# First norm's modulation in four quarters, rows of x reloaded earlier, sums on four column groups

## The reference, cut to what matters

```python
def modulate(h, shift, scale):
    return h * (1 + scale) + shift
def adaln(cond, w, b):                       # w_ada: 1024 x 6144, six pieces of 1024 columns
    return jnp.split(jax.nn.silu(cond) @ w + b, 6, axis=-1)

sh1, sc1, g1, sh2, sc2, g2 = adaln(c, w_ada, b_ada)
csh1, csc1, *_ = adaln(c_ctx, w_ada, b_ada)
hc = modulate(rms_norm(ctx, norm_mix), csh1, csc1)        # 256 tokens of context
s_f, s_b = hgrn2_context_states(*split(hc @ w_in[:, 512:2048]), lb_f, lb_b)
hx = modulate(rms_norm(x, norm_mix), sh1, sc1)            # 512 tokens
mx = token_mix(hx, w_in, w_out, ..., s_f, s_b)            # two gated scans and a convolution
x = x + g1 * mx
hx2 = modulate(rms_norm(x, norm_ffn), sh2, sc2)
x = x + g2 * expert_choice_ffn(hx2, w_router, w_gate, w_up, w_down)   # 16 experts
x = rms_norm(x, norm_final)
# second block: u = rmsnorm(x, g_mix); z = u @ w_in_2, of which 24 columns are the gates of the
# attention branches (sigmoid(zg)); then attention, convolution, FFN, a last gate, a last norm
```

## Time and profile before

| | us |
|---|---|
| median of 3 runs (lowest to highest) | 2087.41 (2086.91 to 2089.4) |
| the profiled execution | 2087.24 |
| its span in the trace | 2085.2 |
| PE busy | 1998.8 (96%) |
| DVE busy / ACT busy / POOL busy | 899.3 / 577.0 / 58.2 |
| DMA | 529.58 MB, mean 254 GB/s |

### The profile page before, as it was taken

One profiled execution on the slowest core, in us unless ns is written; L12 is line 12 of the kernel. 1 busy time (PEld: TensorE's weight loads), 2 busy tenths in 40 slices (PEclk: granted clock), 3 DMA queues, 4 the chain that ended last, 5 costly groups with the idle time before them and its releaser, 6 DMA issues.

```text
span 2085.2 us, 23804 instructions
## 1 busy us (share of the span) xinstructions
PE 1998.8 (96%) x9896; PEld 1247.4 (60%) x9896; DVE 899.3 (43%) x1478; ACT 577.0 (28%) x901; POOL 58.2 (3%) x107
## 2 busy tenths in 40 slices
PE   7999999999999899999999888999999999999998
PEld 5888777543533334242423323776688888888886
DVE  4666683320111111111101101877897656767555
ACT  5434322100100000000000001437725343334445
POOL 1000010000000000000000000005300000000000
PEclk9999999999999999999999999999999999999999
DMA  9462127899999999999999999142132232232322
GB/s 353 162 232 91 41 72 292 362 404 406 428 430 430 430 431 413 429 431 430 431 431 430 431 431 419 56 136 41 41 117 86 81 121 81 91 112 81 111 78 84
DMA packets 111099, 529.58 MB, mean 254 GB/s; under 512 B 15397, under 2 KB 44177, under 8 KB 83345
## 3 DMA queue, kind: packets, MB, share of 16 engines
q1 hardware_dynamic: 110993, 528.07, 62.7%
HBM read 525.95 MB, written 2.10 MB: 253 GB/s over the span
## 4 chain that ended last, share of the span: by engine, by line
PE 91%; DMA 4%; DVE 2%; issue 2%; ACT 0%; SPq 0%; POOL 0%; ACTq 0%; DVEq 0%
PE bank L1099 22%; PE bank L646 12%; PE bank L647 12%; PE bank L648 12%; PE bank L1183 9%; PE bank L1056 3%; PE bank L1073 3%; PE bank L653 3%; PE bank L655 3%; PE bank L657 3%; DMA f<-in_w_gate_dram 3%; PE bank L667 2%; PE bank L1288 1%; PE bank L1397 1%; DMA f<-in_w_in_dram 1%
## 5 line engine op out<-in xcount | busy, mean ns | idle before, releaser
L1099 PE MATMUL bank<-f,high 128*64 128x512 f32 x2048 | 463.5, 600 | 31.4 <-issue 15.3
L646 PE MATMUL bank<-r 128*128 128x512 f32 x920 | 363.4, 395 | 3.4 <-DVE r L2114 2.7
L647 PE MATMUL bank<-r 128*128 128x512 f32 x920 | 359.2, 390 | 0.0
L648 PE MATMUL bank<-r 128*128 128x512 f32 x920 | 358.9, 390 | 0.0
L1099 PEld LDWEIGHTS bank<-f,high 128*64 128x64 f32 x2048 | 147.6, 137 | 317.1 <-issue 299.8
L1183 PE MATMUL bank<-f,high 128*64 128x512 f32 x1024 | 227.5, 600 | 8.3 <-issue 8.3
L2454 DVE SCALAR_TENSOR_TENSOR f<-bank,low,f 128x512 f32<-128x512 f32 x64 | 48.0, 750 | 401.6 <-PE bank L1073 401.2
L1529 ACT ACTIVATE high<-bank 128x512 f32<-128x512 f32 (+3 forms) x95 | 52.1, 579 | 564.0 <-PE bank L667 269.8
L408 DVE TENSOR_TENSOR r<-f,r 128x1024 fp32r<-128x1024 f32 (+2 forms) x167 | 190.9, 1196 | 32.2 <-ACT r L402 32.1
L646 PEld LDWEIGHTS bank<-r 128*128 128x128 f32 x920 | 172.3, 187 | 45.8 <-issue 5.5
L648 PEld LDWEIGHTS bank<-r 128*128 128x128 f32 x920 | 172.4, 187 | 37.6
(11 more groups left out here) (397 smaller groups left out, 2059.5 us busy)
## 6 DMA issues: line engine op xcount, KB each, us to landing
f<-in_w_up_dram SPq DMA_DIRECT2D x58, 2048.0 KB, 20.6
f<-in_w_down_dram SPq DMA_DIRECT2D x56, 2048.0 KB, 20.2
f<-in_w_gate_dram SPq DMA_DIRECT2D x55, 2048.0 KB, 19.1
f<-in_w_up_dram SPq DMA_DIRECT2D x34, 1024.0 KB, 7.2
f<-in_w_in_dram SPq DMA_DIRECT2D x13, 2048.0 KB, 7.8
f<-in_w_down_dram SPq DMA_DIRECT2D x22, 1024.0 KB, 10.7
high<-in_w_ada_dram SPq DMA_DIRECT2D x32, 512.0 KB, 5.4
f<-in_w_gate_dram SPq DMA_DIRECT2D x16, 1024.0 KB, 10.0
```

The costliest lines, as they stand in the source:

```text
L646: pe.matmul(o, wh, xh, start=first, stop=False)
L647: pe.matmul(o, wl, xh, start=False, stop=False)
L648: return pe.matmul(o, wh, xl, start=False, stop=last)
L1099: ins = pe.matmul(o[64 * e:64 * e + 64, :], xsT[p % 2][:, 2 * k + r, 64 * e:64 * e + 64], ws[e](2048 * r + 512 * fc), start=k == 0 and r = ...
```

## The change

Five edits, in program order.

1. The modulation's blocks are cut in four quarters q of 256 features: `early[q]` holds scale and shift of the quarter (rows of 1 KB). SP issues for each q a quarter of ZF, scale q, shift q. `ada_columns(q, a)` multiplies 256 columns, `ada_turned(q)` and `modulation(q)` follow. Quarter 0 comes ahead of the loop over k, quarters 1 to 3 in the middle of k = 0, 2 and 4, turned at k = 1, 3 and 5. Three matmuls on ones (256 columns) stand ahead of the loop. ACT and DVE split ZF's first quarter ahead of the copies of x. Chunk VI waits for quarter 2.
2. ACT's context root stands between tiles 5 and the copy of quarter 3; `pt2` moves behind the first token tile by VI; `ctx_state` is cut in `ctx_turned` and `ctx_state`, with a projection between.
3. The rows of x are reloaded in two halves, after DVE's second `gates` and after the second scan's last products, ahead of the last output weights.
4. `route_sums` takes two d at a time, on four column groups; the two halves are added by a matmul with `fold2` in place of the transpose.
5. The 24 gate columns are one plain float32 product on four column groups (`gate_columns`, weights times gain in `WG`), added by a matmul with `fold4`.

```diff
-            load_ada(2)
-            load_ada(0)
-            load_chunk(0)
-            load_ada(3)
-            load_ada(1)
+            for q in range(4):
+                load_chunk(ZF, [q])
+                sp.dma_start(early[q][:, SCALE], ada_part(SCALE, q)).then_inc(s[f"scale{q}"], 16)
+                sp.dma_start(early[q][:, SHIFT], ada_part(SHIFT, q)).then_inc(s[f"shift{q}"], 16)
...
-            sp.wait_ge(s["pe_ada"], val("pe_ada", 3))
-            sp.wait_ge(s["pe_ada"], val("pe_ada", 1))
+            sp.wait_ge(s["pe_ada"], val("pe_ada", 2))
             load_chunk(1)
...
+            sp.wait_ge(s["v_gla"], val("v_gla", "gates", 1))
+            sp.dma_start(xres[:, 0:2, :], x_v[:, 0:2, :]).then_inc(s["x0"], 16)
+            sp.wait_ge(s["pe_scan"], val("pe_scan", 1, 14))
+            sp.dma_start(xres[:, 2:4, :], x_v[:, 2:4, :]).then_inc(s["x1"], 16)
             sp.wait_ge(s[freed(N1 - 3)[0]], val(*freed(N1 - 3)))
             load_chunk(N1 - 1)
...
-            tokens_turned(0)
-            tokens_turned(1)
-            ada_columns(ada_order[0])
-            tokens_turned(2)
-            ada_turned(ada_order[0])
-            ada_columns(ada_order[1])
+            for t in range(3):
+                tokens_turned(t)
+            ada_columns(0, SCALE)
             tokens_turned(3)
-            ada_turned(ada_order[1])
+            ada_columns(0, SHIFT)
+            ada_turned(0)
+            pe.wait_ge(s["consts"], val("consts", "ones256"))
+            after(3)
+            for _ in range(3):
+                pe.matmul(banks[3][:, 0:256], ident, ones256, start=True, stop=True)
...
             for k in range(8):
-                if k == 2:
-                    ada_columns(3, 0)
-                    ada_columns(1, 1)
-                if k == 3:
-                    ada_turned(3, 2)
-                    ada_turned(1, 3)
+                q, odd = k // 2 + 1, k % 2
+                if odd and q < 4:
+                    ada_turned(q, 2)
...
                 for j in range(4):
+                    if j == 2 and not odd and q < 4:
+                        ada_columns(q, SCALE, q % 2)
+                        ada_columns(q, SHIFT)
...
-            for t in range(2):
-                o = take(("vctx", t), "a_proj", "vctx", t)
-                up(project_tokens(o, VI, t, HCH, HCL), "pe_proj", "vctx", t)
+            o = take(("vctx", 0), "a_proj", "vctx", 0)
+            up(project_tokens(o, VI, 0, HCH, HCL), "pe_proj", "vctx", 0)
+            ctx_turned(0)
+            o = take(("vctx", 1), "a_proj", "vctx", 1)
+            up(project_tokens(o, VI, 1, HCH, HCL), "pe_proj", "vctx", 1)
+            ctx_gate(ZB, 1)
             ctx_state(0)
-            ctx_gate(ZB, 1)
...
-            ctx_state(1)
+            ctx_turned(1)
             for h in range(4):
                 o = take(("q", h), "a_proj", "q", h)
                 up(project(o[:, :], QC, h, UH, UL), "pe_proj", "q", h)
+                if h == 0:
+                    ctx_state(1)
...
+            def route_sums(d0):
+
                 pe.wait_ge(s["v_route"], val("v_route", "wrm"))
-                pe.matmul(st1[0:32, :], WRm[:, d, :], XT[:, d, :], start=d == 0, stop=d == 7)
-                up(pe.matmul(st1[32:64, :], onesD[:, 0:32], sq1[d % 2], start=d == 0, stop=d == 7), "pe_sq", 1, d, 0)
+                for d in (d0, d0 + 1):
+                    g = 64 * (d % 2)
+                    pe.wait_ge(s["sq"], val("sq", 1, d, 0))
+                    pe.matmul(st1[g:g + 32, :], WRm[:, d, :], XT[:, d, :], start=d < 2, stop=d > 5)
+                    up(pe.matmul(st1[g + 32:g + 64, :], onesD[:, 0:32], sq1[d % 2], start=d < 2, stop=d > 5), "pe_sq", 1, d, 0)
...
-                for d in ((0, 1), (2, 3), (4,), (5,))[j]:
-                    route_sums(d)
+                if j < 3:
+                    route_sums(2 * j)
             route_sums(6)
-            route_sums(7)
...
-                ins = pe.transpose(o[:, 64 * t:64 * t + 64], sums[:, 128 * t:128 * t + 128], ident[0:64, 0:64])
+                ins = pe.matmul(o[:, 64 * t:64 * t + 64], sums[:, 128 * t:128 * t + 128], fold2, start=True, stop=True)
...
+            def gate_columns():
+
+                o = take(("ct", 2), "a_z", "ct", 2)
+                pe.wait_ge(s["v_z"], val("v_z", "wg"))
+                for r in range(2):
+                    for g in range(4):
+                        ins = pe.matmul(o[32 * g:32 * g + 32, :], WG[:, 2 * g + r, :], XT[:, 2 * g + r, :],
+                                        start=r == 0, stop=r == 1)
+                up(ins, "pe_z", "ct", 2)
...
-            columns(KVG, 256, 24, 2)
+            gate_columns()
...
+            for q in range(4):
+                ada_tmp(q)
+                if q == 0:
+                    a_divide(a, ZF, [1])
+                rounded_tokens((2 * q, 2 * q + 1))
+                if q < 2:
+                    a_divide(a, ZF, [q + 2])
+                if q == 1:
+                    a.wait_ge(s["v_pre"], val("v_pre", "lbd"))
+                    a.activation(lb0, lb0, ACT.Exp)
+                    up(a.activation(lb1, lb1, ACT.Exp), "a_pre", "lbe")
+                if q == 2:
+                    context_root()
             a_divide(a, VI)
...
+            v.wait_ge(s["hi"], val("hi", KVG, 3))
+            up(v.tensor_tensor(WG[:, :, 0:24], v3(whole(KVG)[:, 0:2240], 8)[:, :, 256:280],
+                               gain12.unsqueeze(2).to_broadcast([P, 8, 24]), ALU.mult), "v_z", "wg")
+            own_wait("v_z")
             v_divide(v, KVG)
...
+            ctx_turned(0)
             v_divide(v, ZB)
+            ada_sums(12, 18)
             ctx_state(0)
-            ada_sums(12, 22)
+            ada_sums(18, 22)
```

More of the change, by code:

```diff
@@ L18 @@
 NEG = -1e30
-DMA_SEMS = (*(f"g{i}" for i in range(6)), *(f"cg{i}" for i in range(4)), *(f"zf{i}" for i in range(4)), "x0", "x1", "rows0", "rows", "small", "ctx", "wple", "ada0", "ada1", "ada2", "ada3", "w0", "w1", "ptok", "gf", "out",
+DMA_SEMS = (*(f"g{i}" for i in range(6)), *(f"cg{i}" for i in range(4)), *(f"zf{i}" for i in range(4)), "x0", "x1", "rows0", "rows", "small", "ctx", "wple", *(f"scale{i}" for i in range(4)), *(f"shift{i}" for i in range(4)), "w0", "w1", "ptok", "gf", "out",
             *(f"m{i}" for i in range(9)), "mx", "my", "mg0", "mg1", "mh0", "mh1", "mq0", "mq1")
@@ L121, in build_program @@
         CP = v3(mem(8 * 32), 8)
-        cursor[0] += 96
+        fold2, fold4 = mem(64), mem(24)
+        cursor[0] += 8
         XT_AT = cursor[0]
@@ L411, in build_program @@
         x_v = I["x"][0].rearrange("(t p) d -> p t d", p=P)
[L412 to L414 removed]
+        early = [own(4096, a_).rearrange("p (a k n) -> p a k n", a=2, k=8)
+                 for a_ in (M + 14336, M + 18432, slot_at[2], slot_at[3])]
+        SHIFT, SCALE = range(2)
         def ada_slot(n):
@@ L436, in sync, with load_chunk @@
         def sync(sp):
-            def load_chunk(c):
+            def load_chunk(c, pieces=None):
                 for i, (dst, src) in enumerate(chunks[c][0](whole(c))):
+                    if pieces and i not in pieces:
+                        continue
                     sp.dma_start(dst, src).then_inc(s[{ZF: f"zf{i}", CG: f"cg{i}"}.get(c, f"w{pair[c]}")], 16)
@@ L782, in tensor @@
                        "pe_proj", "cf", t, half)
-            pe.wait_ge(s["rows"], 16 * len(rows1))
-            o = take(("pt2",), "v_pre", "pt2")
-            up(turn_blocks(o, [stage[:, i, :] for i in range(1, 5)]), "pe_pre", "pt2")
             turn["order"], turn["i"] = [4, 5, 6, 7], 0
@@ L789, in tensor @@
                 up(project_tokens(o, VI, t, UH, UL), "pe_proj", "vtok", t)
+                if t == 0:
+                    pe.wait_ge(s["rows"], 16 * len(rows1))
+                    o = claim(0, ("pt2",), "v_pre", "pt2")
+                    up(turn_blocks(o, [stage[:, i, :] for i in range(1, 5)]), "pe_pre", "pt2")
                 if t == 1:
                     ctx_gate(ZF, 0)
-            for t in range(2):
-                o = take(("vctx", t), "a_proj", "vctx", t)
-                up(project_tokens(o, VI, t, HCH, HCL), "pe_proj", "vctx", t)
+            o = take(("vctx", 0), "a_proj", "vctx", 0)
[4 more added lines that the diff above has]
+            ctx_gate(ZB, 1)
             ctx_state(0)
-            ctx_gate(ZB, 1)
             for h in range(4):
@@ L1275, in to_tokens @@
                 for t in range(4):
-                    ins = pe.transpose(o[:, m * t:m * t + m], ct[i][0:m, 128 * t:128 * t + 128], ident[0:m, 0:m])
+                    z = slice(128 * t, 128 * t + 128)
+                    if i < 2:
+                        ins = pe.transpose(o[:, m * t:m * t + m], ct[i][0:m, z], ident[0:m, 0:m])
+                    else:
+                        ins = pe.matmul(o[:, m * t:m * t + m], ct[i][:, z], fold4, start=True, stop=True)
                 up(ins, "pe_z", "tk", i)
@@ L2217, in vector @@
             v_divide(v, VI)
-            v.wait_ge(s["pe_pre"], val("pe_pre", "pt2"))
```

(4 more changed lines are left out.)

204 lines of the change are left out of this document (95 added, 109 removed).

## The result

The changed kernel takes 2076.54 us in the median of four runs (2075.66 to 2076.88), beside 2087.74 for the kernel before in the same session (2086.91 to 2089.4): a ratio of 0.9944, 95% interval 0.9932 to 0.9956, or 11.2 us less. The profiled execution took 2076.56 us, 10.7 less than that of before, and its span is 10.4 shorter.

A forecast was written before the change was run, and what follows sets the result against it. PE was taken as the bound, with 91% of the chain, and DMA near the expert stage's end. Terms -1.0 + 0.5 - 3.0 - 1.8 - 1.2 - 3.1 = -9.6 from 2087.24 (median 2087.41) gave 2077.7; 8-in-10 range 2074.5 to 2082.5.

The forecast's parts named there:

- VI: First norm: chunk VI issued up to 5 us later behind the quarters' rows; value +0.5, bounds 0 and +2.7.
- The step on the clock: First norm: with ones, PE idles 1.3 us; since 1.83 us of idle kept the clock at 1.00, it stays high.
- The price of that fall: First norm: at the low clock, 1.2 GHz, the first eight products cost 1.6 us more.
- The margin at quarter 3: First norm: ACT's copy of quarter 3, behind the context's root, done at 45; PE wants it at 45.8.
- The rival that rested on it, the first rival: First norm gives nothing: root or VI too late, clock falls, +2.5 + 1.5 instead of -0.5; 2082.2, chance 0.16.
- the quarters double the number of rows in the queue: SP's queue at the first norm: more rows, so VI issued up to 5 us later, landing at 46.5 to 52.
- The folds' estimate of 0.93: Router sums and gates: four float32 products of two instructions replace transposes of 0.43, taking 0.93; +0.5 in each part.
- 2.2 us for eight matmuls at that share: Parts 4 and 5: at overlap share 0.79, eight matmuls take 2.2 instead of 1.92; both parts bring 0.5 less.
- The conclusion (it passes shifts on): Expert stage: whatever PE gains before about 470 us moves the transfer stream and its end by as much.
- From there on the stream runs without a gap: Expert stage: after the empty DMA queues at 470 us, the weight stream has no further gap.
- the last rival: More: clock stays high, quarter 0 starts at 23, all waits go in full; 2074, chance 0.06.

The follow-up runs named there:

- nine traces: One trace each of nine profiled kernels sharing the changed kernel's start; first product between 23.66 and 25.14 us, mean 24.53; the loop behind it takes 31.00 to 31.07.
- all but its start: Kernel before with the change's x reload, sums and gate columns, but the old first norm and old context order: 2080.5 us, ratio 0.9967 to the kernel before.
- the early products: Changed kernel with 30 products of the identity with itself ahead of the first parameter rows and 4 behind them: 2074.76 us, ratio 0.9938 to the kernel before.
- the delay ahead of it: Changed kernel with 16 more products on ones (7.2 us) ahead of the second block of output products, at about 345 us: 2083.53 us, ratio 0.9982.
- the delay in pair 3: Changed kernel with the same 7.2 us of extra products on ones put in expert pair 3: 2083.36 us, ratio 0.9976 to the kernel before.

## Why the prediction was right

I forecast 2077.7 in a range of 2074.5 to 2082.5; 2076.54 was measured. Term by term, in us:

| part | forecast | before against after | undone by itself, in the trace |
|---|---|---|---|
| 1, first norm, with VI | -0.5 | -0.3 | not tried alone |
| 2, context | -3.0 | -3.55 | -3.0, without `pt2` |
| 3, rows of x | -1.8 | -1.9 | -3.6 |
| 4, sums | -1.2 | -1.3 | -1.3 |
| 5, gates | -3.1 | -3.1 | -3.5 |

*Part 1.* The first product was forecast at 24.4, and the mean of nine traces is 24.5; the loop was forecast at 30.9 and took 31.0. The step on the clock was decisive, and its outcome right: with 1.19 us of idle time the clock stayed at 1.00 in all eleven starts with the ones, and in the three without them it was at 0.50. Its reason was weaker than it looked. It went from one case, 1.83 us at 320 us, to a rule by length, and the expert stage has a wait of 1.81 us behind which the clock fell (last section). That 1.19 us was safe is shown by the runs, and did not follow from the row. The price of that fall I had at 1.6 us; it is 2.1 to 2.5, because the low level outlasts the eight products and takes the second quarter's 32 instructions too. The loop's end was forecast at 55.3, and the nine have 55.56 in the mean. The two profiled executions that carry the table show only 0.3 gained, but they are one draw each of a start that varies by more than a microsecond. The old start was traced twice, with its loop's end at 56.34 and at 58.02; against the mean of the nine that is 0.8 and 2.5. The median difference between the whole change and all but its start (4.2) less the context's 3.55 leaves 0.7. So part 1 is measured no better than between a few tenths and 2.5 us, with the medians at 0.7, against -0.5 forecast with VI. It is the least certain line of the table, and that the line agrees so well is partly luck.

*The margin at quarter 3.* Forecast at 0.8 us and called the tight one. The copy started at 45.57 and was done when PE came to the turn at 46.92, without a wait; the early products shifted everything by two microseconds and still PE did not wait. The rival that rested on it got no support. For VI, forecast up to 5 us late at a price of 0.5, the issue moved by 1 us and the price was nothing: SP held the context's issue for 3.20 us, not 5.01. My step "the quarters double the number of rows in the queue" overrated this by as much.

*Part 2.* The mechanism was right and the size too small: I counted each wait by its 0.99 of idle time. From start to start each costs 1.24. Three of them are 3.7. With 0.16 more at the two states, and less the 0.3 paid for the interrupted rows of products, that is the 3.55 of the stretch.

*Part 3.* Right in the comparison at hand (the waits went, 0.2 came back for DVE's banks, against 0.5 forecast). But its worth depends on the clock behind the wait: undone in the changed kernel it cost 3.6 in the trace.

*Parts 4 and 5.* Sized from two rows of the same shape in other places, and right within 0.2 each. Four column groups overlapped in full (16 instructions in 1.91 us), where the Trainium skill (TensorE: Matmul & The Clock Gate, "Measured speedup vs the span model") gives 2.38 of 3 for three column tiles; the trace decides for full overlap at 512 columns in float32. The folds' estimate of 0.93 was near: 1.08 and 0.97. The prediction's 2.2 us for eight matmuls at that share is a slip: 1.92 / 0.79 is 2.4.

*The expert stage.* The conclusion (it passes shifts on) was right, 7.1 us in and 7.1 out, and the delay ahead of it confirmed it. The step "From there on the stream runs without a gap" was wrong: I had looked at stretches around 470 and 1225 us, and the last place where PE holds the transfers is near 810 us. Had one of the parts lain between 470 and 810 us, I would have written its gain off, and the delay in pair 3, which cost 6.8 of its 7.2 us, shows that this would have been wrong.

*The range.* It was said to take in the last rival, but that one stood at 2074, below the range's 2074.5. And the first rival went to +1.5 for VI, called an upper bound, where the bound of that term was +2.7. Neither came into play.

## What to carry to other kernels

To know what a gain in a stage bound by transfers is worth, scan the whole stage for dips in the transfer rate, in short stretches: up to the last dip at which the matrix engine is busy, an edit of it counts in full, and behind it hardly at all. Price a wait from start to start, not by its idle time: 0.99 us of idle time cost 1.24. And look at the clock behind it: where it fell, that cost 1.5 to 2.5 us more, and a few products that nobody reads, put into the gap, took it back at the start. The length of a wait alone does not tell whether the clock falls. And compare traces from a point behind the start, where runs of the same code differ.

## What the runs showed of the hardware

- The price of idle time of TensorE is not linear. Behind 1.19 us of it (eleven starts) and 1.83 us (at 320 us, before) the clock stayed at the high level; behind 2.34, 2.59 and 2.71 us (twice) products ran at the low one, 1.2 GHz, for 3 to 6 us. In the run with the old reload of x it fell only after PE had begun again (0.99 in the stretch 318:320, 0.50 in 320:322).
- Yet the length of the idle time does not decide. At the same place of the expert stage, PE is idle for 1.81 us in the changed kernel and for 1.82 in the one with early products; behind the first the clock is at 0.50, behind the second at 1.00. And in the run with the old reload of x it stays at 1.00 behind 3.03 us. Idle time and the stretch behind it, in this order:
```profile
672.32 0.63 PE L670 MATMUL bank<-low,high 128*128 128x128 f32 x4 [1.81 <-DVE high L2518]
674.00:676.00 2.00, 2.00 (x11) 2.00 (x11) 1.11 (x2) 0.00 (x0) 0.00 (x0) 0.50 0.96 410
...
670.22 0.63 PE L670 MATMUL bank<-low,high 128*128 128x128 f32 x4 [1.82 <-DVE high L2522]
671.00:673.00 2.00, 2.00 (x19) 2.00 (x19) 2.00 (x4) 0.54 (x1) 0.00 (x0) 1.00 1.04 442
...
713.98 3.66 PE L1114 MATMUL bank<-f,high 128*64 128x512 f32 x16 [3.03 <-DMA f<-in_w_gate_dram]
714.00:716.00 2.00, 2.00 (x10) 0.86 (x12) 0.00 (x0) 0.00 (x0) 0.00 (x0) 1.00 1.07 459
```
What else decides, these traces don't show.
- The column of the granted clock can mislead at a program's start. For the changed kernel it has 1.00 here,
```profile
12.00:14.00 2.00, 1.98 (x10) 1.98 (x11) 2.00 (x4) 1.99 (x5) 0.00 (x0) 1.00 1.09 387
```
while the 24 transposes took 5.38 us in this kernel, and 2.84 in the version with early products under the same 1.00. The lengths of the instructions, not that column, gave the version with early products. The Trainium skill (TensorE: Matmul & The Clock Gate, "Seeing it yourself") warns that the trace's records of the clock have been unreliable. Here no record is seen to be wrong, but one is missing: the changed kernel's trace has its first record of the clock at 17.8 us, and the column shows 1.00 for the time ahead of it. At 320 us and at 24 us the column and the instructions agree.
- 384 to 398 GB/s in the first norm with the rows of w_ada at 1 KB, against 409 with rows of 2 KB: 3 to 6% less; the single stretch of the earlier trace rows had 6%. It cost nothing, since PE was never behind a landing.
- The early products have a cost of their own: 60 instructions lasted until 11.29 us, and the turn of the first parameter rows, at 10.19 in the changed kernel, moved to 11.13. A smaller number of them might give some tenths more; that was not tried.
